# Weights and moving operands at one place modulo 512 bytes, and sixteen unread products in the split type

## The reference

```python
u = rms_norm(x, ln1[i]) * (1.0 + scale1) + shift1
mix = mixer_sublayer(u, w_in[i], ...)                 # u @ w_in, conv, scan, ... @ w_o
x = x + gate1 * mix
hid = jnp.square(jax.nn.relu(u2 @ w_up[i]))
x = x + gate2 * (hid @ w_down[i])
...
x = x + 0.5 * swiglu(rmsnorm(x, g_ffn1[l]), w1_gate[l], w1_up[l], w1_down[l])
```

## Time and profile before

| | before |
|---|---|
| median of two runs | 2297.05 us |
| span of the profiled execution | 2287.7 us |
| TensorE busy (matmul) | 2237.3 us, 98% |
| TensorE weight loads | 1829.0 us, 80% |
| VectorE, ScalarE, GpSimd busy | 1320.4, 863.7, 4.5 us |
| TensorE's share of the chain that ended last | 87% |
| mean granted clock of TensorE | 0.993 |

### The profile page before, as it was taken

The page is one execution under the profiler, slowest core; times in us unless marked ns, Lnnn a source line. Parts: engine busy times, 40 slices in busy tenths (PEclk is TensorE's granted clock), DMA queues, the critical chain, the costliest instruction groups (busy, mean ns, idle before and its releaser), DMA issues.

```text
span 2287.7 us, 28544 instructions
## 1 busy us (share of the span) xinstructions
PE 2237.3 (98%) x10872; PEld 1829.0 (80%) x10872; DVE 1320.4 (58%) x1835; ACT 863.7 (38%) x1223; POOL 4.5 (0%) x8
## 2 busy tenths in 40 slices
PE   7999999999999999999999999999989899999998
PEld 5888888887888888888878888889868667888887
DVE  5577777777673475433475344355777766434344
ACT  5655555543222342322342222234445444212124
POOL 0000000000000000000000000000000000000000
PEclk9999999999999999999999999999999899999999
DMA  7323233224543243323222222223121002232321
GB/s 263 114 75 105 96 98 104 92 74 162 169 154 103 92 129 115 101 90 99 92 92 92 92 92 93 92 92 91 49 65 38 19 32 79 92 97 96 103 83 65
DMA packets 208140, 222.08 MB, mean 97 GB/s; under 512 B 9413, under 2 KB 200330, under 8 KB 205994
## 3 DMA queue, kind: packets, MB, share of 16 engines
q1 hardware_dynamic: 206362, 210.26, 28.5%
q10 hardware_dynamic: 1680, 10.49, 1.1%
HBM read 218.57 MB, written 2.16 MB: 96 GB/s over the span
## 4 chain that ended last, share of the span: by engine, by line
PE 87%; DVE 7%; ACT 3%; issue 2%; DMA 1%; ACTq 0%; DVEq 0%
PE G L551 24%; PE G L552 24%; PE G L553 24%; PE G L587 2%; PE G L589 2%; PE G L588 2%; DVE wlo L1806 1%; PE X L739 1%; ACT whi L1159 1%; PE G L1024 1%; DMA araw<-in_w_ada 1%; PE X L1041 1%; PE X L1007 1%; PE X L1031 1%; DVE score L2688 1%
## 5 line engine op out<-in xcount | busy, mean ns | idle before, releaser
L551 PE MATMUL G<-ahi,whi 128*128 128x512 f32 x1496 | 603.0, 403 | 4.1 <-DVE alo L2782 1.4
L552 PE MATMUL G<-alo,whi 128*128 128x512 f32 x1496 | 592.2, 396 | 0.0
L553 PE MATMUL G<-ahi,wlo 128*128 128x512 f32 x1496 | 591.9, 396 | 0.0
L1806 DVE TENSOR_TENSOR wlo<-raw,whi 128x2048 fp32r<-128x2048 f32 x176 | 403.3, 2292 | 240.2 <-ACT whi L1159 236.9
L1159 ACT ACTIVATE whi<-raw 128x2048 fp32r<-128x2048 f32 x176 | 335.5, 1907 | 454.9 <-PE G L553 434.3
L551 PEld LDWEIGHTS G<-ahi,whi 128*128 128x128 f32 x1496 | 282.9, 189 | 72.3 <-issue 2.4
L553 PEld LDWEIGHTS G<-ahi,wlo 128*128 128x128 f32 x1496 | 282.6, 189 | 67.2
L552 PEld LDWEIGHTS G<-alo,whi 128*128 128x128 f32 x1496 | 282.9, 189 | 66.7 <-issue 2.2
L551 PE MATMUL G<-hhi,whi 128*128 128x512 f32 x784 | 310.2, 396 | 0.7 <-DVE wlo L1806 0.7
L552 PE MATMUL G<-hlo,whi 128*128 128x512 f32 x784 | 309.6, 395 | 0.0
L553 PE MATMUL G<-hhi,wlo 128*128 128x512 f32 x784 | 309.5, 395 | 0.0
(11 more groups left out here) (410 smaller groups left out, 2783.6 us busy)
## 6 DMA issues: line engine op xcount, KB each, us to landing
raw<-in_w_in SPq DMA_DIRECT2D x43, 1024.0 KB, 5.1
raw<-in_w_up SPq DMA_DIRECT2D x38, 1024.0 KB, 5.3
raw<-in_w_down SPq DMA_DIRECT2D x32, 1024.0 KB, 5.1
raw<-in_w_gate SPq DMA_DIRECT2D x22, 1024.0 KB, 5.1
braw<-in_w_ada SPq DMA_DIRECT2D x12, 1024.0 KB, 5.1
raw<-in_w_in SPq DMA_DIRECT2D x20, 512.0 KB, 4.5
araw<-in_w_ada ACTq DMA_DIRECT2D x8, 1024.0 KB, 17.7
bc<-acum_dram SPq DMA_DIRECT2D x8, 1024.0 KB, 6.9
```

The costliest lines, as they stand in the source:

```text
L551: pe.matmul(bank[:], wh[:, j, f], rh[:, j, :], start=(j == 0), stop=False)
L552: pe.matmul(bank[:], wh[:, j, f], rl[:, j, :], start=False, stop=False)
L553: last = pe.matmul(bank[:], wl[:, j, f], rh[:, j, :], start=False, stop=(j == k - 1))
L1806: tt(wlo[s][:], raw[s][:], r32(whi[s][:]), ALU.subtract).then_inc(lo_split, 1)
```

## The change

Three things change, all in `build`.

1. The layout. A `fixed` tensor `to_weights` of 32 words (128 bytes) is put ahead of the stage tensors, `PAD` grows from 12 to 124 words (48 to 496 bytes), and the scan stage gets a filler `to_line` of 112 words behind `pre`. Nothing reads or writes these. This is where the tensors start, in bytes within a partition, modulo 512, as the allocator places them:

| tensors | before | after |
|---|---|---|
| `raw`, `whi`, `wlo`, `xT`, `ones`, `ident` | 128 | 128 |
| `ahi`, `alo`, `hhi`, `hlo`, `bhi`, `blo`, `clo`, `lhi`, `llo`, `pacc`, `xin`, `araw`, `braw` | 0 | 128 |
| `chi`, `xwhi`, `xwlo`, `qc`, `yhi`, `ylo`, `cv`, `xf`, `seg`, `bc`, `xdt`, `xw` | 64 | 128 |

Blocks of activations are 2048 bytes apart, blocks of weights 1024, and the two halves of a unit 512, so every 128 x 128 or 128 x 512 block of a tensor starts at its tensor's place modulo 512. (The one exception is the first unit, 32 columns wide, whose blocks are 128 bytes apart.)

2. The five unread products ahead of the three transposes, in float32, become sixteen in the split type, with one tensor `unread`, all ones, on both sides. Four of the sixteen read the moving side as it lies, four read one word 512 times, four read every second word, and four read the first 32 words 16 times.

3. GpSimd sets `unread` (128 x 1024 words) behind `epsT`, and TensorE waits for it (`unread_ready`) ahead of the sixteen.

```diff
-PAD = 12
+PAD = 124
+TO_WEIGHTS, TO_LINE = 32, 112
...
+        fixed("to_weights", [P, TO_WEIGHTS])
         split_a = (("ahi", [P, KB, T], F32R), ("alo", [P, KB, T], F32R))
...
         ahi, alo, xin, *araw = phase(*split_a, ("xin", [P, TB, D]), *((f"araw{u}", [P, UNIT]) for u in range(8)),
-                                     ("adacc", [P, UNIT]))
+                                     ("adacc", [P, UNIT]), ("behind_dtw", [P, 768]), ("unread", [P, 2 * T], F32R))
+        unread, _ = araw.pop(), araw.pop()
         adacc = araw.pop()
...
-        (pacc, pre, cv, xf, zs, xdt, xw, btok, sm, seg, bc, states, yf, yhi, ylo, dts, dtw) = after_a(
-            "_s", ("pacc", [P, KB, T]), ("pre", [P, 4, 3 + T]), ("cv", [P, 4, T]), ("xf", [P, 4, T]),
+        (pacc, pre, _, cv, xf, zs, xdt, xw, btok, sm, seg, bc, states, yf, yhi, ylo, dts, dtw) = after_a(
+            "_s", ("pacc", [P, KB, T]), ("pre", [P, 4, 3 + T]), ("to_line", [P, TO_LINE]), ("cv", [P, 4, T]), ("xf", [P, 4, T]),
...
             pe.wait_ge(x_ready, 1)
-            keep_clock(5, xT[:, 0, :])
+            pe.wait_ge(unread_ready, 1)
+            for src in (unread[:, 0:T], unread[:, 0:1].broadcast_to([P, T]), unread[:, 0:2 * T:2],
+                        unread[:, 0:32].unsqueeze(1).broadcast_to([P, T // 32, 32])):
+                for _ in range(4):
+                    pe.matmul(X[2][:], unread[:, 0:P], src, start=True, stop=True)
             pe.wait_ge(dskip_ready, 1)
...
             pool.memset(epsT[:], EPS).then_inc(gone, 1)
+            pool.memset(r32(unread[:]), 1.0).then_inc(unread_ready, 1)
             pool.wait_ge(vec_landed, 16 * VECS)
```

More of the change, by code:

```diff
@@ L258, in build @@
         x_free = [sem(f"x_free{b}") for b in range(4)]
-        gone = sem("gone")
+        gone, unread_ready = sem("gone"), sem("unread_ready")
         dve_step, act_step = sem("dve_step"), sem("act_step")
```

## The result

The changed kernel takes 2254.1 us (2254.04 and 2254.16), against 2297.05 before: 0.9825 of it, 95% interval 0.9802 to 0.9847, 43 us less. In a later set of runs (`changed_again`) it took 2253.4 against 2295.7, 0.9822 (0.9795 to 0.985). I had forecast no change, 2297.8 us. Instead the rival came true that I had given a third of the chances, faster by part or more.

What follows compares the result with a forecast made beforehand. TensorE's distance between large matmuls, 7512 x 233.3 ns = 1753 us of 2287.7, was taken as the bound. 2287.7 + 0.4 + 0.3 = 2288.4 us, plus 9.35 for the runs, gave 2297.8 us, range 2249 to 2325.

Steps and rivals of the forecast that it cites:

- faster by part or more: Large matmuls: 1.5 to 6 ns less each, 2251 to 2286 us, chance 0.19; over 6 ns less, chance 0.14.
- What bounds the kernel: TensorE: the distance between starts of 7512 large matmuls, 233.3 ns each, makes 1753 of 2287.7 us.
- I take 0 ns: Large matmuls: the new layout would leave the distance between starts as it was, at 233.3 ns.
- Not by a rule of distance: All matmuls: places matter by 1 to 5 ns, but 64 bytes apart gave 233.3 as well as 113.3 and 117.8.
- The bounds: Every matmul: at best 5.5 ns less (118.8 to 113.3, the best drop seen), at worst 5.5 ns more.
- `chi` +0.4 us, `xwhi` +0.3 us: Two operands losing their odd place: `chi` from 229.2 to 233.3 ns, `xwhi`/`xwlo` to 118.8 ns.
- The cost of the unread products: Start of the kernel: sixteen for five cost 0, hidden by a wait until 30.54 us; bound +1.2 us.
- The first four alone answer the question for the split type: Unread products reading as it lies: 215 or 240 ns in the first four would prove the forecast wrong.
- 9.35 us over this profiled execution: Whole kernel: the runs' median of 2297.05 us lies this far above the profiled span, added to 2288.4 us.
- the place is the stall: Rival, all matmuls: both sides at one place stop disturbing each other; 2261, 2249 or 2145 us; chances 0.19 and 0.14.
- collision: Rival, L551 to L553: weight load and moving operand read one place at once; 2325 or 2346 us; chances 0.09 and 0.06.
- The rhythm: Rival, large matmuls: history sets 232 or 234 ns, not the place; 7.5 us either side, inside the 0.52 forecast.

Runs made afterwards that it cites:

- changed_again: The changed kernel itself, run again beside the kernel before: 2253.4 us, 0.9822 of it.
- distance: The changed kernel with 48 groups of 24 unread matmuls for the sixteen, weights d bytes behind the moving operand: 226.7 ns at d = 0, 232.5 at 128.
- distance3: Like `distance`, with groups of 18 in another order, so that different places stood ahead: d = 0 always 226.7 ns, d = 16 226.7 or 233.3.

## Why the prediction was wrong, point by point

- **What bounds the kernel**: right. TensorE's distance between large matmuls set the time; 7512 of them at 5.9 ns less on average (226.9 for 232.8) are the whole gain.
- **"I take 0 ns" for the layout**: the step that failed. It measured 5.9 ns less on average over all (43.3 us / 7333): from 232.4 to 233.2 by stage, and 229.0 for `chi`, down to 226.7 to 227.0. It rested on the last block of the first unit, 237 ns with both sides at one place. I had called it the weakest step, and it was: `distance` shows that weights 32 columns wide run at about 231 at each of the five places tried, so those rows could say nothing on weights of 128 columns. The 237 also take in the change to the first full tile.
- **"Not by a rule of distance"**: wrong. `yhi` at 64 apart (233.3) and `xwhi` at 64 apart (113.3 and 117.8) are not a contradiction. 64 apart is as slow as 128 for 512 columns (233.3), and away from 0 the rhythm depends on history. The row that pointed the right way was `chi`, 4.1 ns faster than the rest, and I let it stand as an oddity. How much of its 4.1 ns the place makes is open, since the group laid out like it took 231.2.
- **The bounds**: 5.5 ns, taken from 256 columns, was a little short for 512 columns (5.9 on average, 6.6 between the rows shown) and had the wrong sign for 256 (1.2 ns more). Carried over to all 8800 they gave 2249, near the measured 2254 by luck: one error is too little on 7512 matmuls, the other a gain on 1300 that was a loss. The 0.80 for a change of less than 2% came true by size alone too (1.75%), since I had given the layout nothing.
- **`chi` +0.4 us, `xwhi` +0.3 us**: `chi` gained (229.2 to 226.7), `xwhi` went to 120.0 as a loss of 0.2 to 0.6 us. The sign of the first was wrong, both are too small to matter.
- **The cost of the unread products**: right. One pattern doubled (every second word, 450 to 469 ns), not both, and the transposes started at 30.87 us, near the 30.8 worked out. The memset took 0.95 us for my 0.9.
- **"The first four alone answer the question for the split type"**: wrong. They lay at one place and were 315, 229, 233 and 236 ns apart. By that sign I would have been right, while the kernel's own matmuls ran at 226.7. A group at d = 0 needs up to ten matmuls to settle, and four were too few. The count in the stretch, 443 for 430, was the sign that held.
- **Loads, VectorE, ScalarE**: right; VectorE's busy time went from 1320.4 to 1318.8 us, ScalarE's from 863.7 to 864.3.
- **"9.35 us over this profiled execution"**: wrong. What lies around the span is 1.8 us (2254.16 against 2252.4 for the same run). The other 7.5 go with the clock: 0.993 in the profiled execution, 0.986 to 0.988 in the runs of 2297 to 2300 us.
- **The rival "the place is the stall"** came true near its lower prices: not 18.3 ns, but 5.9 on average on 512 columns, and 2254 us between its 2261 and its 2249. The "disturbing" that it gave as the reason is not shown. Float32 products at one place, which I cited for it, were no evidence: `distance3` has them at 429 ns at either place. The rival "collision" can be laid aside for these forms: with weights 128 columns wide that are read word by word, no group of d = 0 on a 32-byte line was slower than at other places for 512 columns, though with 256 columns it is (120.0). The rhythm, which I had as a third rival worth 7.5 us, exists (d = 16 and 240), but does not decide the kernel.
- **By the Trainium skill's two read ports**, "TensorE: Matmul & The Clock Gate", Part 2, the layout would be worth nothing. The measurement decides: 43 us. With a one-word moving operand the place made no difference (218.8 and 218.7 ns), with one that is read from end to end it did. Whether what is lost is read bandwidth, no run shows.
- **The N / 2.4 + 2.5 ns** that the prediction takes from the Trainium skill's "Back-to-back issue gap": that section gives it for an isolated matmul, and Part 1 of the same page for back-to-back ones. The trace's split type stays above its 215.8 ns in every group: the lowest settled distance with 512 columns was 217.8 (runs of 8 words).

What stays open is the mechanism. Shown is where the distance always came to 226.7: split type, weights of 128 columns without a gap, a moving operand of 512 columns that is read on, both on 32 bytes and at one place modulo 256. That two reads stop hindering each other does not fit, since with weights that are one word 128 times, it is 231.7 and not 226.7 or less. Why the common place should be faster than that, no run tells. Nor was it tried whether data other than ones changes the groups, though the kernel's own matmuls on real data run at the same 226.7.

## What to carry to other kernels

Measure the distance between starts of the kernel's main matmul by stage. If it differs between stages of one form, or lies above that of another type, look at where the operands start. A row of unread matmuls at the start of the kernel, one line for each pair of places, gives the whole table in one run. Make the groups long: 24 were enough, four were not. They forecast the kernel to 0.1 ns where they had its three matmuls by turns with one operand out of place, or all at one place (231.1 against 231, 226.7 against 226.7), but missed `chi` before the change by 2 ns (231.2 against 229.2), so try the change in the kernel too. A row from another form (32 columns, 256 columns, float32) says nothing about this one; all three misled me here. One operand out of place in three can cost most of the gain: `wlo` cost 30.8 us of it.

## What the runs showed of the hardware that I had not expected

- The same product of the split type takes 226.7 ns at one place modulo 256 bytes and mostly 228.3 to 233.8 elsewhere; near 0 it depends on what ran ahead (d = 16: 226.7 or 233.3). With 256 columns one place is at the slow end (120.0 against 117.1 to 118.2 at d = 32 to 192).
- Both operands off the 32-byte grid cost 3 to 11 ns per matmul of 512 columns even at d = 0 (230.0 to 237.8). Reading every second word doubles the time, and repeated runs of 16 or 32 words (241.8, 236.7) are slower than reading on.
- The spread of this kernel's runs (2286.8 to 2300.1 us before) goes with the granted clock (0.993 to 0.986). In two profiles of the changed kernel the difference lies in the attention stage: 361.7 us at a clock of 0.97, 368.1 at 0.94.
- A row of matmuls at one place took up to ten of them to reach its 226.7 ns.
